# One decoder layer with a mixture of experts: all twelve weight slots of an expert staged, in 2 MB transfers, and the prompt output summed in PSUM

## The reference

```python
logits = x2 @ w_router + b_router              # x2: rms-normalised rows, 288 x 1024
top_vals, top_idx = lax.top_k(logits, 4)       # 4 of 32 experts
gates = softmax(top_vals)
# per expert e, over the rows that chose it:
gu = xb @ w_up[e] + b_up[e]                    # 1024 -> 2048
gate, up = min(gu[:, :1024], 7), clip(gu[:, 1024:], -7, 7)
act = (up + 1) * (gate * sigmoid(1.702 * gate))
y += row_gate * (act @ w_down[e] + b_down[e])  # 1024 -> 1024
out = rmsnorm(x + y, norm_final_g)
```

## Time and profile before

| what | value |
|---|---|
| median of three runs | 1273.46 us (1272.34 to 1274.46) |
| profiled execution, its own time | 1271.02 us |
| its span, first to last instruction | 1269.2 us |
| PE busy | 1152.5 us, 91% |
| VectorE (DVE) busy | 676.7 us, 53% |
| GpSimd (POOL) busy | 653.9 us, 52%, of it 623.8 us in the copies of L524 |
| ScalarE (ACT) busy | 244.0 us, 19% |
| mean transfer rate over the span | 354 GB/s |
| mean granted TensorE clock | 0.972 |

### The profile page before, as it was taken

One profiled execution on the slowest core, in us unless ns is written; L12 is line 12 of the kernel. 1 busy time (PEld: TensorE's weight loads), 2 busy tenths in 40 slices (PEclk: granted clock), 3 DMA queues, 4 the chain that ended last, 5 costly groups with the idle time before them and its releaser, 6 DMA issues.

```text
span 1269.2 us, 30932 instructions
## 1 busy us (share of the span) xinstructions
PE 1152.5 (91%) x11113; PEld 586.8 (46%) x11114; DVE 676.7 (53%) x1256; ACT 244.0 (19%) x487; POOL 653.9 (52%) x709
## 2 busy tenths in 40 slices
PE   8999999999999989799797998997997879979895
PEld 7777777775444334243332443432433324434332
DVE  2999984121755635545342557553554445535534
ACT  2012124001222212122121221221221212212122
POOL 1012300000566858749671687586585756857863
PEclk9999999999999999999898999998998989989998
DMA  9974443336999999999999799999999999999996
GB/s 263 349 242 129 163 129 117 114 142 278 380 385 397 396 422 422 421 422 422 422 422 422 282 400 424 422 422 422 422 422 422 422 422 422 422 422 422 422 422 277
DMA packets 94539, 448.91 MB, mean 354 GB/s; under 512 B 8502, under 2 KB 42870, under 8 KB 45315
## 3 DMA queue, kind: packets, MB, share of 16 engines
q1 hardware_dynamic: 94078, 447.21, 87.8%
q10 hardware_dynamic: 437, 1.39, 0.3%
HBM read 447.00 MB, written 2.42 MB: 354 GB/s over the span
## 4 chain that ended last, share of the span: by engine, by line
PE 60%; DMA 18%; DVE 17%; issue 3%; DVEq 1%; ACT 1%; POOL 0%; SPq 0%; POOLq 0%; ACTq 0%
PE banks L1372 21%; DMA ring<-in_w_down 17%; PE banks L1382 13%; DVE staging L803 8%; PE banks L1167 8%; PE banks L1089 5%; PE banks L1147 4%; PE banks L1126 3%; PE banks L1283 2%; PE banks L1133 2%; PE banks L1156 1%; DMA staging<-in_w_up 1%; DVE hT L1036 1%; DVE hT L1029 1%; DVE staging L812 1%
## 5 line engine op out<-in xcount | busy, mean ns | idle before, releaser
L524 POOL COPY ring<-staging 128x1024 f32<-128x1024 f32 x620 | 623.8, 1053 | 472.0 <-PE banks L1372 372.4
L1372 PE MATMUL banks<-ring,hT 128*32 128x512 f32 x3328 | 414.8, 604 | 12.7 <-DVE hT L779 7.5
L330 DVE TENSOR_TENSOR xt<-xt,banks 128x1024 f32<-128x1024 f32 x106 | 128.7, 1215 | 371.7 <-PE banks L1147 371.7
L1382 PE MATMUL banks<-ring,hT 128*32 128x256 f32 x3328 | 229.1, 395 | 73.3 <-DMA ring<-in_w_down 64.4
L1382 PEld LDWEIGHTS banks<-ring,hT 128*32 128x32 f32 x3328 | 109.6, 114 | 249.7 <-issue 136.3
L1167 PE MATMUL banks<-hT,ring 128*128 128x288 f32 x768 | 188.4, 406 | 0.3 <-ACT hT L561 0.3
L1372 PEld LDWEIGHTS banks<-ring,hT 128*32 128x32 f32 x3328 | 104.8, 111 | 149.9 <-issue 106.8
L1167 PEld LDWEIGHTS banks<-hT,ring 128*128 128x128 f32 x768 | 145.1, 190 | 39.7 <-issue 0.4
L683 ACT COPY WT<-banks 128x256 f32<-128x256 f32 x52 | 19.4, 372 | 533.8 <-PE banks L1382 533.8
L803 DVE SCALAR_TENSOR_TENSOR staging<-staging 128x256 f32<-128x256 f32 x240 | 107.4, 522 | 0.0
L762 DVE TENSOR_SCALAR WT<-slot_ids,prod 128x32 f32 x156 | 81.5, 581 | 0.0
(11 more groups left out here) (245 smaller groups left out, 737.0 us busy)
## 6 DMA issues: line engine op xcount, KB each, us to landing
staging<-in_w_up SPq DMA_DIRECT2D x248, 1024.0 KB, 18.5
ring<-in_w_down SPq DMA_DIRECT2D x66, 1024.0 KB, 11.1
staging<-in_w_down SPq DMA_DIRECT2D x62, 1024.0 KB, 18.4
ring<-in_w_in SPq DMA_DIRECT2D x24, 1024.0 KB, 10.3
ring<-in_w_up SPq DMA_DIRECT2D x8, 1024.0 KB, 4.8
ring<-in_w_branch_b SPq DMA_DIRECT2D x4, 1024.0 KB, 5.4
ring<-in_w_branch_a SPq DMA_DIRECT2D x4, 1024.0 KB, 4.9
ring<-in_w_out SPq DMA_DIRECT2D x4, 1024.0 KB, 5.0
```

Of the source, the lines that this page charges most:

```text
L330: nc.vector.tensor_tensor(dst, dst, rows, ALU.add).then_inc(y_added, 1)
L524: ins = nc.gpsimd.tensor_copy(ring[:, k, half], staged[k][:, half])
L1372: ins = mm(UP[g * BLK:(g + 1) * BLK, :], xT[:, k, :], ring[:, k, g * 512:(g + 1) * 512], start=k == 0, stop=k == UP_SLOTS - 1)
L1382: ins = mm(DN[q * BLK:(q + 1) * BLK, 0:256], actT[:, f % 4, f // 4, :], ring[:, UP_SLOTS + j, h * D + q * 256:h * D + (q + 1) * 256], star ...
```

## The change

All six units (12 slots) of an expert are staged. A transfer is one unit of 2 MB: 16 KB in a row for each partition, in place of 8 KB. SyncE's order is then PE's: units 0 to 5 of the expert after, each when GpSimd has emptied it; only the last unit of the last expert goes straight into the ring. GpSimd copies 12 slots per expert; PE still waits slot by slot (the count rises by 8 for each slot copied).

The prompt rows of the output are summed in PSUM: `start_rows` puts the residual rows there by a product with the identity, each `combine` accumulates on it, and VectorE's adds and `y_added` go. At the end ScalarE squares both tiles out of PSUM under one wait, one root serves both, and VectorE scales out of PSUM.

`stage` is no longer kept through the expert stage: prompt rows are gathered from `xt` unscaled, and the selection matrix carries the scale as a second operation. The buffers of the mixing part and of routing move into the six staged units; so the staging loads of expert 1 wait for these to be free, the last unit for `items_known`. Since a partition now holds other rows of a weight matrix, the orders in which rows, biases and activations are turned change (pairs and fours), and the norm's weights are loaded once more in that order (`ffn_rows`, 4 KB).

```diff
+            def unit_source(e, u):
+                if u < UP_UNITS:
+                    return a["w_up"][0, bass.ds(e, 1), u * 256:(u + 1) * 256, :].rearrange("e (p h) n -> p (e h n)", p=P)
+                lo = (u - UP_UNITS) * 512
+                return a["w_down"][0, bass.ds(e, 1), lo:lo + 512, :].rearrange("e (p h) n -> p (e h n)", p=P)
+            def load_unit(e, u):
+                sp.dma_start(ring[:, 2 * u:2 * u + 2, :].rearrange("p s n -> p (s n)"), unit_source(e, u)
+                             ).then_inc(unit_full[u], 16)
+            def load_staged(e, u):
+                sp.dma_start(staged[u], unit_source(e, u)).then_inc(staged_full[u], 16)
+            def load_staged_again(place, us):
+                after = sp.value_load(order[0:1, bass.ds(place + 1, 1)], min_val=0, max_val=NE - 1)
+                for u in us:
+                    sp.wait_ge(unit_full[u], place * 16 + 16)
+                    load_staged(after, u)
...
             sp.wait_ge(ya_evac, 2 * KC)
-            for k in range(UP_SLOTS):
-                load_staged(1, k)
+            sp.wait_ge(v_stored, 16)
+            for u in range(UP_UNITS):
+                load_staged(1, u)
             sp.wait_ge(*mix_block_used(MIX_BLOCKS - 1))
-            for k in range(UP_SLOTS, SLOTS):
-                load_slot(0, k)
-            for k in range(UP_SLOTS, 2 * STAGED):
-                load_staged(1, k)
-            sp.wait_ge(before_known, 1)
-            with sp.Fori(1, NE - 1) as place:
...
-                load_staged_again(place, after, range(2 * AHEAD))
-                load_last_slots(here, before)
-                load_staged_again(place, after, range(2 * AHEAD, 2 * STAGED))
+            for u in range(UP_UNITS, UNITS):
+                load_unit(0, u)
+            load_staged(1, UP_UNITS)
+            sp.wait_ge(items_known, 1)
+            load_staged(1, UNITS - 1)
+            with sp.Fori(1, NE - 2) as place:
+                load_staged_again(place, range(UNITS))
+            load_staged_again(NE - 2, range(UNITS - 1))
...
+            sp.wait_ge(down_used, before * DOWN_SLOTS + DOWN_SLOTS)
+            load_unit(last, UNITS - 1)
...
+            def copy_slot(u, h):
                 for c in range(2):
...
+                ins.then_inc(unit_full[u], 8)
+            def copy_expert(place, us):
+                before = pool.value_load(items_before[0:1, bass.ds(place - 1, 1)], min_val=0, max_val=MAX_ITEMS)
+                for u in us:
+                    pool.wait_ge(staged_full[u], place * 16)
+                    for h in range(2):
...
+                        copy_slot(u, h)
...
+                for tt in range(2):
+                    V.tensor_scalar(sel[:, tt, :], slot_ids[:, bass.ds(rank0, BLK)],
+                                    rankm[:, tt, bass.ds(expert, 1)], ss[:, 4 + tt:5 + tt], ALU.is_equal, ALU.mult)
...
-            def add_before(i, tt):
-                dve.wait_ge(combined, i * NT + (tt + 1))
-                add_output(dve, row_out[tt], tt) if tt < 2 else add_quarters(dve, DN[:, 256:512])
+            def add_sample(i):
+                dve.wait_ge(sample_combined, i + 1)
+                V.tensor_tensor(xq[:], xq[:], sample_out, ALU.add).then_inc(sample_added, 1)
...
+            def start_rows():
+                for q in range(QN):
+                    mm(bank[4 + q].rearrange("p (t n) -> p t n", t=2), ident[:], x_cols[:, q], start=True, stop=False)
+            def combine(tt, last=False):
+                for q in range(QN):
+                    ins = mm(y_rows[tt][:, q, :],
+                             combT[q * BLK:(q + 1) * BLK, tt * P:(tt + 1) * P],
+                             out_sb[q * BLK:(q + 1) * BLK, :], start=False, stop=last)
+                return ins
...
+            def up(k, half, full):
+                pe.wait_ge(unit_full[k // 2], (half, full)[k % 2])
...
+            def down(j, half, full):
+                pe.wait_ge(unit_full[UP_UNITS + j // 2], half if j == 0 else full)
...
+            act.wait_ge(rows_combined, 1)
             for tt in range(2):
+                nc.scalar.activation(squares[tt], y_rows[tt], ACT.Square, accum_out=ss[:, tt:tt + 1]
                                      ).then_inc(squared3, 1)
+            act.wait_ge(squared3, 2)
+            root(ss[:, 4:6], ss[:, 0:2], 1.0 / D, rooted2)
```

More of the change, by code:

```diff
@@ L126, in hybrid_layer @@
         order = sb("order", [1, NE], I32)
[L127 to L152, removed]
+        staging = sb("staging", [P, UNITS, UNIT])
@@ new lines, in hybrid_layer, with part @@
+        staged = [staging[:, u, :] for u in range(UNITS)]
+        areas = [staging[:, 0:UP_UNITS, :].rearrange("p u n -> p (u n)"), staged[UP_UNITS], staged[UNITS - 1]]
+        MIXED, LAST_MIXED, ROUTED = range(3)
+        taken = [0, 0, 0]
+        def part(area, n, rows=P):
+            lo = taken[area]
+            taken[area] = lo + n
+            assert taken[area] <= areas[area].shape[1]
+            return areas[area][0:rows, lo:lo + n]
+        big, R1, R2, R4 = part(MIXED, KC * CB), part(MIXED, KC * T), part(MIXED, KC * T), part(MIXED, KC * T)
@@ L153, in hybrid_layer @@
+        below = part(ROUTED, P)
+        below_q = part(ROUTED, QN * NS, NS).rearrange("p (q t) -> p q t", q=QN)
+        wr = part(ROUTED, KC * NE).rearrange("p (k e) -> p k e", k=KC)
+        br = part(ROUTED, NE)
+        key_bias = part(ROUTED, NE, NE)
+        rank_at = part(ROUTED, NE - FIXED, NE)
+        movable, first_place = part(ROUTED, 1, NE), part(ROUTED, 1, NE)
         xs_rows = spb[0:NS].rearrange("p g i -> p (g i)")
@@ L185, in carve @@
             return regs[region][0:rows, lo:lo + n]
+        squares = [regs["hT"][:, tt * D:(tt + 1) * D].rearrange("p (q n) -> p q n", q=QN) for tt in range(2)]
         xT = carve("hT", KC * BLK).rearrange("p (k t) -> p k t", k=KC)
@@ L194, in hybrid_layer @@
         combT = carve("WT", 2 * P + NS)
[L195 to L206, removed]
-        item_place, item_expert, item_begin, item_column = (carve("prod", 1) for _ in range(4))
+        lx = part(ROUTED, NT * (NE + 8)).rearrange("p (t e) -> p t e", t=NT)
+        lr = part(ROUTED, NT * (NE + 8)).rearrange("p (t e) -> p t e", t=NT)
+        top8 = part(ROUTED, NT * 8).rearrange("p (t e) -> p t e", t=NT)
+        want8 = part(ROUTED, NT * 8).rearrange("p (t e) -> p t e", t=NT)
+        mask = part(ROUTED, NT * NE).rearrange("p (t e) -> p t e", t=NT)
+        need = part(ROUTED, MAX_ROUNDS - 1, NE)
+        key_row, less = (part(ROUTED, NE, NE) for _ in range(2))
+        placed = part(ROUTED, 2 * NE, NE)
+        key_col, rank, place, blocks = (part(ROUTED, 1, NE) for _ in range(4))
+        ends, started, begins = (part(ROUTED, NE) for _ in range(3))
+        item_place, item_expert, item_begin, item_column = (part(ROUTED, 1) for _ in range(4))
         fing, fingq = ring[:, 0, 0:D], ring[:, 0, D:D + 256]
-        stageq = stage[:, 2, 0:256]
+        x_cols = xt[:].rearrange("p t (q n) -> p q t n", q=QN)
         banks = ctx.enter_context(nc.psum_tensor("banks", [P, 8, 512], F32))
@@ L438, in _ @@
+            load_staged(1, UP_UNITS)
[4 more added lines that the diff above has]
+            load_staged_again(NE - 2, range(UNITS - 1))
             before = sp.value_load(items_before[0:1, NE - 2:NE - 1], min_val=0, max_val=MAX_ITEMS)
-            here = sp.value_load(order[0:1, NE - 1:NE], min_val=0, max_val=NE - 1)
-            load_last_slots(here, before)
+            last = sp.value_load(order[0:1, NE - 1:NE], min_val=0, max_val=NE - 1)
```

273 lines of the change are left out of this document (119 added, 154 removed).

## The result

The changed kernel takes 1246.63 us (median, 1245.65 to 1248.65), the kernel before 1273.96 us beside it (1272.34 to 1275.87): ratio 0.9783, 95% interval 0.9771 to 0.9796. The profiled execution took 1247.34 us with a span of 1245.5, 23.7 us less than that of before (1271.02 and 1269.2). Forecast were 1249 for the median and 1247.0 for the profiled execution.

A forecast was written before the change was run, and what follows sets the result against it. The expert stage was taken as bound by its weight stream, PE second. From 1271.0 us profiled, -17.1 - 10.2 + 0.3 + 3.0 = -24.0 gave 1247.0, plus 2.4 a median of 1249 us; range 1238 to 1268.

The forecast's parts named there:

- Staged slots in order: Expert stage, stretches from 330 and 690 us: twelve staged slots in PE's order recover 17.1 of 20.6 us lost.
- the split behind the sum: Expert stage: of 19.9 us of lead, PE's order gives 14.9 and the two added slots 5.0.
- 2 MB transfers: Weight stream from 332.8 us: 16 KB runs reach 428.5 GB/s, gaining 13.6 us, of which three quarters, 10.2, were taken.
- The start: Ahead of the first weights: one added 4 KB load costs its issue time on SyncE, +0.3 us.
- The end: After slot 7 lands: copies, last bias, norm and PE's pace in the last block together cost +3.0 us.
- The copy's +2.0: At the end, slots 6 and 7 land together and are copied in turn, so up(7) starts 2.0 us later.
- the last bias, the norm and PE's pace: At the end: -0.5 us before the last bias, +0.5 for the norm, 1 for PE paced by arrivals.
- The 2.4 us added for the median: Whole kernel: the median was put 2.4 us above the profiled execution, as before the change, giving 1249 us.
- (1): Weight stream: longer runs move no faster, the rate stays at 422 GB/s; 1259 us, chance 0.25.
- (3): DMA queues from 332 us: 16 KB packets are served worse than two of 8 KB; 1301 us, chance 0.10.
- (2): Expert stage: PE replaces the stream as bound, as GpSimd's longer copy bursts lock VectorE; 1263 us, chance 0.10.
- (4): Weight stream: the pauses move elsewhere and the rate stands; 1273 us, chance 0.05.

The follow-up runs named there:

- direct: Changed kernel with every expert's last unit loaded straight into the ring again, behind three up units of the next expert: ratio 1.0012 to the kernel before.
- alt64: Changed kernel with each staged unit loaded by two 1 MB transfers, even then odd partitions, runs still 16 KB: 1247.98 us, ratio 0.9805 to the kernel before.
- slack: Changed kernel with seven transposes of each block done twice, 1.16 us more TensorE work per block: 1261.62 us, ratio 0.9909 to the kernel before.
- runs8: Changed kernel with each staged unit loaded by two 1 MB transfers by column halves, so runs are 8 KB again: ratio 0.9888 to the kernel before.
- start: Changed kernel with the load and two transposes of the second norm layout moved behind the first projections: 1246.15 us, ratio 0.9792 to the kernel before.
- start_end: Changed kernel with those transposes moved and the last expert's up units 2 and 3 loaded straight into the ring: 1245.77 us, ratio 0.9793 to the kernel before.

## Why the prediction was right

By its own terms, of the profiled executions:

- *Staged slots in order*, forecast -17.1: 20.6 us lost before, 4.1 + 0.4 after: -16.1. The stretch from 690 closed but for 0.4 us, as forecast; of the first one 4.1 us stay where I left 3.5. One premise failed: the reloads don't go out as early as they did, but from 339.34 in place of 332.81. Of these 6.5 us 3.9 are the later start, and a unit is free only when both of its slots are copied. What went wrong besides is the split behind the sum: from `direct` the order weighs 20 us, and the two slots 8.9, once units of two are handed over and the last unit waits for all four down products, and the change needs both.
- *2 MB transfers*, forecast -10.2: at 428.5 the 379.6 MB take 885.9 us in place of 899.5: -13.6. The line through runs of 1 KB and 8 KB held in full, and taking three quarters of it was too careful. The rate is the run's, not the transfer's (alt64). At 428 to 429 GB/s it lies between the 425 and the ceiling of 435 that the Trainium skill gives (DMA: Bandwidth & Descriptors, section "Where 436 GB/s comes from").
- *The start*, forecast +0.3: +3.9. I had priced the added 4 KB load by its issue and forgot that PE transposes what it brings, twice, ahead of its first projection. That is 0.8 us, and the rest is TensorE at its lower clock for longer, in two stretches that before doesn't have at these places. The sum had no term for it, and by `slack` it doesn't come in every execution of this start.
- *The end*, forecast +3.0: from the landing of slot 7 to the end of the span 24.2 us before (1269.2 - 1245.02), 26.3 after (1245.5 - 1219.17): +2.2. The copy's +2.0 came out (4.35 less 2.38); what I added for the last bias, the norm and PE's pace, 1 us together, is 0.2. The down products took 3.70 us in both, so that the 1 us for PE's pace was not there.

Sum: -16.1 - 13.6 + 3.9 + 2.2 = -23.6, measured -23.7. From the load of the first expert's down weights to the landing of slot 7, 928.1 us became 898.3, which is 29.7 less and what the first two terms give together. The forecast of -24.0 is right in its mechanism and signs, but that it is this near is luck: the rate's 3.4 us and the start's 3.6 us cancel. The 2.4 us added for the median did not hold: the profiled execution after lies 0.7 us above its median, not below.

The rivals: (1) is refuted by runs8 and alt64, (3) by 428. (2) is not what happened, since the stream decides, but its mechanism is there. The prediction had priced one line of VectorE, up to 0.8 us in a block; the product of line 1036 can be held as long and already was, in 22 blocks. The five instructions grew by 0.6 us on average, and PE stood 0.5 to 0.9 us from deciding, where the prediction's 15.9 to 16.7 against 17.4 left 0.7 to 1.5. (4), that pauses move elsewhere, is what `direct` shows for the change without its order.

## What to carry to other kernels

Where a stream of weights sets the time, fetch them in the order in which they are used and into buffers that no late consumer holds, before making the transfers larger: with the old order put back, the larger ones and all the rest of the change were no faster than the kernel before (`direct`), though in that order runs of 16 KB still beat runs of 8 KB by 0.60%. When the stream gains, compute the next bound anew with the engines' instructions at the length that they have beside each other (16.7 us a block here, not 15.9), and follow every byte added ahead of the first product to the instructions that unpack it. Read TensorE's rate from the count of its products, too, where the trace has no record of its clock.

## What the runs showed of the hardware

A transfer that covers partitions 0 to 63 or 64 to 127 alone moved 214 GB/s at a full DMA share, one over every other partition 428, both in runs of 16 KB and 1 MB each: which partitions a transfer holds counts, not how many. The Trainium skill (SBUF — State Buffer, section "Door 1: The DMA port swizzle") has a map of partitions to 16 ports by which either half reaches 8 of them and the even partitions all; the two rows agree.

A load's rate grew once more from runs of 8 KB to 16 KB, 422 to 428 GB/s, and 1 KB, 8 KB and 16 KB lie on one line of 9.5 ns and 0.0368 ns per byte for a run on one of the 16 engines (348 GB/s at 1 KB).

TensorE began at half its rate in every trace. The first record of its granted clock, 1.00, begins 9.9 to 11.1 us after the span's start in four traces (before, `start`, `start_end`, `slack`), where the first 64 products of the projections took 15.76 us, and at 15.3 to 18.4 us in the other ten, where they took 17.2 to 18.1. What sets the moment is not shown; of two kernels with the same start, one can have it early and one late. A view that prints 1.00 before the first record says nothing of the clock; the count of products in a window does (three per us, then six).
